# Attention values as the stationary operand in column tiles, an earlier last attention group, and a reordered output projection in a decoder-layer kernel

## The reference

```python
z = x @ w_in                       # q, k, v of 8 attention heads; q, k, v, o and gates of 4 mLSTM heads
s = q_a . k_a * HEAD_DIM_A ** -0.5 - slope[h] * dist          # only the 128 keys chosen per query
prob = softmax(s);  y_a = prob @ v_a                          # 8 heads of 64: 512 columns
y_m = sigmoid(o_m) * group_norm(mlstm(silu(conv(q_m)), silu(conv(k_m)), v_m, i, f))   # 4 heads of 128
mix = concat([y_a, y_m]) @ w_out                              # 1024 x 1024
x = layer_norm(alpha * x + mix, ln1)
ffn = hierarchical_moe(x)          # a router chooses 2 of 32 experts per token
x = layer_norm(alpha * x + ffn, ln2)
return x + sigmoid(x @ w_g) * (p @ w_p)
```

## Time and profile before

| what | value |
|---|---|
| three executions | 720.65, 721.0, 724.42 us; median 721.0 us |
| profiled execution | 722.4 us, of it 720.6 us span |
| PE busy | 648.5 us, 90% of the span |
| DVE busy | 348.8 us, 48% |
| ACT, POOL busy | 178.9 us, 168.3 us |
| mean granted TensorE clock | 0.957 of full speed |
| the chain that ended last | PE 64%, DMA 6%, SP queue 5%, DVE 5% of the span |
| DMA | 151.21 MB, mean 210 GB/s |

### The profile page before, as it was taken

How to read it: one execution, slowest core, us unless ns; L and a number is a source line. 1 busy time by engine, 2 the same in 40 slices (tenths; PEclk the granted TensorE clock), 3 DMA queues, 4 the chain that set the end, 5 groups by cost and what they waited for, 6 DMA issues and landing times.

```text
span 720.6 us, 10045 instructions
## 1 busy us (share of the span) xinstructions
PE 648.5 (90%) x3782; PEld 454.1 (63%) x3782; DVE 348.8 (48%) x803; ACT 178.9 (25%) x344; POOL 168.3 (23%) x175
## 2 busy tenths in 40 slices
PE   4999999999999999799626999999999997868997
PEld 3768887878787787688523555555555553423785
DVE  3379998657564576616762112211111111117846
ACT  5165132324323233410210111111111111024311
POOL 7206414001010000351103233333333332110100
PEclk9959999989999999999876999999999999998999
DMA  6402301203100500077296888999999999987003
GB/s 239 189 1 89 146 30 61 115 0 115 62 1 0 234 1 0 1 264 300 95 399 250 280 321 297 410 415 417 414 414 414 414 414 416 419 333 302 3 0 117
DMA packets 30438, 151.21 MB, mean 210 GB/s; under 512 B 7308, under 2 KB 7564, under 8 KB 16432
## 3 DMA queue, kind: packets, MB, share of 16 engines
q1 hardware_dynamic: 23984, 142.08, 49.9%
q0 software_dynamic: 6400, 8.42, 3.3%
HBM read 148.36 MB, written 14.68 MB: 226 GB/s over the span
## 4 chain that ended last, share of the span: by engine, by line
PE 64%; DMA 6%; SPq 5%; DVE 5%; issue 2%; ACT 1%; DVEq 0%; POOLq 0%; ACTq 0%
PE bank L1890 15%; PE bank L1599 9%; PE bank L1600 8%; PE bank L1601 8%; PE bank L1905 8%; SPq L449 5%; DMA raw<-in_w_exp_dram 4%; PE bank L1679 3%; PE bank L1954 2%; PE bank L1700 2%; PE bank L1880 2%; PE bank L1688 2%; PE bank L1729 1%; PE bank L1897 1%; PE bank L1720 1%
## 5 line engine op out<-in xcount | busy, mean ns | idle before, releaser
L1514 DVE COPY rows_x<-bank 128x128 f32<-128x128 f32 x40 | 11.6, 291 | 195.1 <-PE bank L1897 195.1
L1599 PE MATMUL bank<-w_hi,a_hi 128*128 128x384 f32 (+1 forms) x240 | 88.0, 367 | 5.9 <-POOL w_lo L578 2.9
L1601 PE MATMUL bank<-w_hi,a_lo 128*128 128x384 f32 (+1 forms) x240 | 86.5, 361 | 0.0
L1600 PE MATMUL bank<-w_lo,a_hi 128*128 128x384 f32 (+1 forms) x240 | 86.4, 360 | 0.0
L1599 PE MATMUL bank<-a_hi,w_hi 128*128 128x512 f32 (+1 forms) x176 | 71.1, 404 | 11.3 <-POOL w_lo L571 9.9
L666 POOL DMA_INDIRECT pair_dram<-rows_x,row_put x40 | 40.5, 1013 | 166.4 <-ACT rows_x L908 166.4
L1890 PE MATMUL bank<-raw,rows_x 128*64 128x256 f32 x544 | 65.6, 393 | 6.6 <-DMA raw<-in_w_exp_dram 5.0
L1600 PE MATMUL bank<-a_lo,w_hi 128*128 128x512 f32 (+1 forms) x176 | 69.5, 395 | 0.0
L1601 PE MATMUL bank<-a_hi,w_lo 128*128 128x512 f32 (+1 forms) x176 | 69.2, 393 | 0.0
L1890 PEld LDWEIGHTS bank<-raw,rows_x 128*64 128x64 f32 x544 | 40.2, 142 | 36.0 <-issue 14.7
L1890 PE MATMUL bank<-slots,rows_x 128*64 128x256 f32 x512 | 58.5, 380 | 3.2 <-DMA slots<-in_w_exp_dram 3.2
(11 more groups left out here) (250 smaller groups left out, 1032.6 us busy)
## 6 DMA issues: line engine op xcount, KB each, us to landing
raw<-in_w_exp_dram SPq DMA_DIRECT2D x42, 1024.0 KB, 13.1
slots<-in_w_exp_dram SPq DMA_DIRECT2D x36, 1024.0 KB, 12.1
rows_x<-in_w_exp_dram SPq DMA_DIRECT2D x12, 1024.0 KB, 13.9
raw<-in_w_in_dram SPq DMA_DIRECT2D x19, 512.0 KB, 4.0
raw<-in_w_wide_dram SPq DMA_DIRECT2D x4, 1536.0 KB, 6.8
y<-in_w_exp_dram SPq DMA_DIRECT2D x6, 1024.0 KB, 14.8
raw<-in_w_out_dram SPq DMA_DIRECT2D x4, 1024.0 KB, 9.2
raw<-pair_dram SPq DMA_DIRECT2D x4, 1024.0 KB, 9.1
```

The costliest lines, as they stand in the source:

```text
L1599: t_.matmul(o, lh, rh, start=first, stop=False)
L1600: t_.matmul(o, lh, rl, start=False, stop=False)
L1601: return t_.matmul(o, ll, rh, start=False, stop=last)
```

## The change

1. **pv.** The values (128 keys x 64 columns of one head) become stationary and the transposed probabilities move, 128 columns; the two heads go to the two column halves of the array and write the two halves of the partitions of `attn_bank`. The result comes out transposed, one column block of y for 512 tokens. There are 4 calls per group, in steps 4 and 5, in place of 8 in steps 2 to 5.
2. **normalise.** Row sums lie along partitions only before the transposition, so the probabilities are multiplied by the inverse sums before `turn`, in a new DVE function at the start of steps 1 to 4; `turn` waits for it. `attn_out` is a plain copy. The y of attention needs no `turn_y` any more.
3. **Table.** `ATTEND` is [12, 17, 22, 26].
4. **Output projection.** The quarters come as 2, 0, 1, 3. The four mLSTM blocks are turned one by one between the `token_major` blocks, which start as soon as attention's columns are split; tiles 0 and 1 are ended before tiles 2 and 3, and the transposition of a normalised tile (`turn_first`) stands between later blocks.
5. **DVE's normalisation** is written out by hand; centring and scaling are apart. The router's weights are rounded and split later. SP loads quarter 3 only after the last pv.

```diff
+        prob_t0 = scratch[:, 5120:6400]
...
-        row_sum = small[:, 8:16].rearrange("p (t h) -> p t h", h=2)
+        row_sums = [small[:, o:o + 8].rearrange("p (t h) -> p t h", h=2) for o in (8, 96)]
...
-        ATTEND = [12, 18, 24, 30]
+        ATTEND = [12, 17, 22, 26]
...
-        OUT_Q = [0, 2, 1, 3]
-        TURNS = [0, 4, 1, 5, 2, 6, 3, 7]
+        OUT_Q = [2, 0, 1, 3]
+        TURNS = [0, 1, 2, 3, 5, 4, 6, 7]
...
             for q in range(4):
+                if q == 3:
+                    sp.wait_ge(s_pv, NT * NG)
...
             pool.wait_ge(s_olo, 1)
+            pool.wait_ge(s_norm, 8 * NG)
             split_out(1)
...
+            for i in range(NG):
+                y_high(i)
+            work(NG, 0)
+            round_out(1)
+            for i in range(NG, 2 * NG - 1):
+                y_high(i)
+            round_out(2)
+            round_out(3)
+            y_high(2 * NG - 1)
...
+            def normalise(g, j):
+                hh, b = 2 * j // NT, 2 * j % NT
+                dve.wait_ge(s_exp, 8 * g + 2 * j + 2)
+                v.reciprocal(row_inv[:, b:b + 2, hh:hh + 1], row_sums[g % 2][:, b:b + 2, hh:hh + 1]).then_inc(s_yinv, 1)
+                dve.wait_ge(s_yinv, 4 * g + j + 1)
+                for e in range(2):
+                    part = prob[:, e, 0:(b + e + 1) * P]
+                    v.tensor_scalar(part, part, row_inv[:, b + e, hh:hh + 1], None, ALU.mult).then_inc(s_norm, 1)
...
-                v.reciprocal(row_inv, row_sum).then_inc(s_yinv, 1)
...
+                dve.wait_ge(s_pv, NT * (g + 1))
+                v.tensor_copy(y_a[:, g, :], attn_bank[:, :]).then_inc(s_ya, 1)
...
             def attention(g, j):
+                if 1 <= j <= 4:
+                    normalise(g, j - 1)
...
+            for i in range(NG):
+                y_low(i)
+            lstm_variance(HM - 1)
+            for i in range(NG, 2 * NG - 1):
+                y_low(i)
+            lstm_out(HM - 1)
+            y_low(2 * NG - 1)
...
+            mixed(2, 0)
+            mixed(2, 1)
+            norm_centre(2, s_ln)
+            mixed(3, 0)
+            norm_scale(2, s_ln, s_rs)
+            low_first(1)
+            mixed(3, 1)
+            norm_centre(3, s_ln)
+            low_first(2)
+            norm_scale(3, s_ln, s_rs)
+            low_first(3)
...
             def turn(g, u):
                 U, b = 8 * g + u, u % NT
-                pe.wait_ge(s_exp, U + 1)
+                pe.wait_ge(s_norm, U + 1)
...
+            def pv(g, b):
+
+                pe.wait_ge(s_probt, 8 * g + NT + b + 1)
+                pe.wait_ge(s_evac, step_no(g, TALL + b) + 1)
+                if b == 0 and g:
+                    pe.wait_ge(s_ya, g)
                 for s in range(b + 1):
...
+                    for hh in range(2):
+                        rows = slice(hh * DA, (hh + 1) * DA)
+                        mm = t_.matmul(attn_bank[rows, b * P:(b + 1) * P], v_a[:, g % 2, s, rows],
+                                       turned(hh * NT + b)[:, s * P:(s + 1) * P], start=s == 0, stop=s == b)
...
-                    if 2 <= j <= 5:
-                        pv(g, 2 * j - 4 + e)
+                    if 4 <= j <= 5:
+                        pv(g, 2 * j - 8 + e)
...
+            pe.wait_ge(s_evac, NSTEP - 1)
+            turn_y(4)
+            work(NG, 0)
+            pe.wait_ge(s_evac, NSTEP)
+            turn_y(5)
...
+            token_major(2, 2, 0)
+            pe.wait_ge(s_ylo, 6)
+            turn_y(6)
+            token_major(2, 3, 0)
+            token_major(2, 1, 0)
             pe.wait_ge(s_ylo, 7)
...
+            token_major(0, 0, 1)
+            token_major(0, 1, 1)
             turn_y(7)
+            token_major(0, 2, 1)
             pe.wait_ge(s_ylo, NK)
...
+            mlstm_part(0)
+            token_major(0, 3, 1).then_inc(s_wo, 1)
+            mlstm_part(1)
...
+            token_major(1, 2, 2).then_inc(s_wot, 1)
+            turn_first(0)
+            token_major(3, 2, 3).then_inc(s_wot, 1)
+            token_major(1, 3, 2).then_inc(s_wot, 1)
+            turn_first(1)
+            token_major(3, 3, 3).then_inc(s_wot, 1)
+            turn_first(2)
+            pe.wait_ge(s_wrs, 2)
+            route(0)
+            turn_first(3)
```

More of the change, by code:

```diff
@@ L357, in hybrid_layer, with turned @@
         TB_FIXED, TB_REST, TB_BLOCK = 9, 8, 9
+        def turned(u):
+            hh, b = u // NT, u % NT
+            return prob_t[:, b % 2, 0:(b + 1) * P] if hh else prob_t0[:, MO[b]:MO[b] + (b + 1) * P]
         def group(m, q):
@@ L861, in _, with y_high @@
                     work(grp, j)
[L863 to L874 removed]
+            def y_high(i):
+                k = TURNS[i]
+                if k < NG:
+                    act.wait_ge(s_proj, NSTEP)
+                    act.wait_ge(s_ya, k + 1)
+                else:
+                    act.wait_ge(s_yt, i - 3)
+                a.activation(a_hi[:, k, :], y_columns(k), ACT.Copy).then_inc(s_yhi, 1)
+            for i in range(NG):
[7 more added lines that the diff above has]
+            y_high(2 * NG - 1)
             def copy_logits(half):
@@ L885, in _ @@
                              turned_1[u][:, :].rearrange("p (k c) -> p k c", k=4), ACT.Copy).then_inc(s_x1hi, 1)
+                if u == 1:
+                    act.wait_ge(s_wr, 16)
+                    act.wait_ge(s_wo, 2)
+                    a.activation(w_hi[:, WR_AT:3 * GW], wr_raw.rearrange("p k c -> p (k c)"), ACT.Copy)\
+                        .then_inc(s_wrs, 1)
                 if u == 5:
@@ L1285, in norm_apply, with norm_scale @@
                                        op1=ALU.mult).then_inc(done, 1)
+            def norm_scale(t, done, ready):
+                m = mine[:, t, :]
                 dve.wait_ge(done, 2 * t + 1)
@@ L1297, in turned_low, with mixed, low_first @@
                     .then_inc(lo, 1)
-            def norm_tiles(prepare, ready, done, weights, banks, hi, lo):
-                for t in range(NT + 1):
-                    if t < NT:
-                        prepare(t)
-                    if t:
-                        if t == 1:
-                            dve.wait_ge(weights, 32)
-                        norm_apply(t - 1, done, ready)
-                    if t >= 2:
-                        turned_low(2 * t - 4, banks, hi, lo)
-                        turned_low(2 * t - 3, banks, hi, lo)
-                turned_low(2 * NT - 2, banks, hi, lo)
-                turned_low(2 * NT - 1, banks, hi, lo)
+            def mixed(t, half):
+                dve.wait_ge(s_xn[t], 16)
+                dve.wait_ge(s_wot, 2 * t + half + 1)
+                residual(t, half)
+                dve.wait_ge(s_r, 2 * t + half + 1)
+                norm_stats(t, half, s_bn)
+                if half:
+                    norm_variance(t, s_bn, 3 * t + 2, s_ve)
+            def low_first(t):
+                for u in (2 * t, 2 * t + 1):
+                    turned_low(u, turned_1, s_x1hi, s_x1lo)
+            mixed(0, 0)
+            mixed(0, 1)
+            dve.wait_ge(s_lnw, 32)
+            norm_centre(0, s_ln)
+            norm_scale(0, s_ln, s_rs)
+            mixed(1, 0)
+            mixed(1, 1)
+            norm_centre(1, s_ln)
+            norm_scale(1, s_ln, s_rs)
+            low_first(0)
             dve.wait_ge(s_wrs, 1)
@@ L1316, in _ @@
                             w_hi[:, WR_AT:3 * GW].bitcast(F32), ALU.subtract).then_inc(s_wrs, 1)
-            def mixed(t):
-                dve.wait_ge(s_xn[t], 16)
-                for half in range(2):
-                    dve.wait_ge(s_wot, 2 * t + half + 1)
-                    residual(t, half)
-                    dve.wait_ge(s_r, 2 * t + half + 1)
-                    norm_stats(t, half, s_bn)
-                norm_variance(t, s_bn, 3 * t + 2, s_ve)
-            norm_tiles(mixed, s_rs, s_ln, s_lnw, turned_1, s_x1hi, s_x1lo)
+            mixed(2, 0)
[9 more added lines that the diff above has]
+            low_first(3)
             n = [0]
@@ L1789, in token_major @@
                     k = 4 * (q % 2) + kk
+                    if place == 0 and t == 2:
+                        pe.wait_ge(s_ylo, k + 1)
                     mm = three(o[:, :], a_hi[:, k, t * P:(t + 1) * P], a_lo[:, k, t * P:(t + 1) * P],
@@ L1842, in turn_logits, with turn_first @@
                     mm.then_inc(s_rp, 1)
-            for t in range(NT):
+            def turn_first(t):
                 pe.wait_ge(s_ln, 2 * t + 2)
                 turn_tile(t, turned_1, s_x1t, s_x1lo)
-                if t == 2:
-                    pe.wait_ge(s_wrs, 2)
-                    route(0)
+            token_major(1, 2, 2).then_inc(s_wot, 1)
[8 more added lines that the diff above has]
+            turn_first(3)
             turn_logits(0)
```

115 lines of the change are left out of this document (37 added, 78 removed).

## The result

The change made the kernel slightly slower, by 0.4%. Over 22 executions of each, the median is 726.8 us against 723.0 us for the kernel before; the ratio is 1.0043, with a 95% interval of 1.0027 to 1.0059. In the 22 the kernel before lies 2 us above the median of the first three. 713.0 us and a gain of 8 had been forecast, with a range up to 720.5.

What follows compares the result with a forecast made beforehand. PE was taken to bound the last three projection groups, with waits on DVE behind them. The four stretches summed, +11.4 - 16.7 + 4.0 - 6.8 = -8.1 us, taking the 721.0 us median to 713.0, range 706.5 to 720.5.

Steps and rivals of the forecast that it cites:

- P: The last three projection groups, 121.98 to 278.78 us: forecast to grow by 11.4 us.
- The rival that two tiles would not overlap: In pv, column-tile records follow each other at 0.108 us, so nothing is gained: 720.6 us, no change; chance 0.08.
- A: Behind the last projection, up to w_out: 22.82 us becomes 6.1, a gain of 16.7.
- N: The first normalisation, behind w_out until turn_first of tile 3: 13.85 us becomes 7.1, a gain of 6.8.
- Waits in P: In the last three projection groups, turn waits for normalise's reciprocal and scalings: +5.5 us, bounds 2 and 12.
- Step 16: In the projection, step 15 to 16: a wait of 1.6 us appears if the low-clock stretch that hides it goes.
- The 0.5 us booked as a gain: In the last three projection groups, lstm_qk's wait on convolve_end goes, no longer colliding with attn_out: -0.5 us.
- O: The output projection w_out, to 345.73 us: 44.13 us becomes 48.1, +4.0; POOL's later power costed at nothing.
- The other term of O: In w_out, PE waits 1.6 us for the split of mLSTM block 2.
- The clock: Low-clock stretch in the last three projection groups costs 3.4 us; its going gains 3.4, another one costs 3.4.
- Waits at all 16 turning steps: Normalise finds no cover in the projection, 1.15 us a step: 18.4 in place of 5.5, 725.9 us; chance 0.07.
- Small delays eat it: Another low-clock stretch (3.4 us), DVE late in more steps (2 to 4), quarter 3 or POOL late (2): 717.5 to 724.5; chance 0.08.

Runs made afterwards that it cites:

- the power edit: Changed kernel, but POOL takes the last mLSTM head's power before splitting w_out's second quarter: 0.9978 to the kernel before, 720.9 us.
- pv first alone: Changed kernel with pv ahead of and between the two transpositions of step 4, nothing else: 0.9921 to the kernel before.
- the three edits: Changed kernel with POOL's power before the split, pv ahead of and between step 4's transpositions, convolution end behind attention in steps 9 and 16: 0.9801, 710.6 us.
- the convolution edit: Changed kernel with the power edit, plus DVE's end of a convolution behind attention in steps 9 and 16: 0.9926 to the kernel before.

## Why the prediction was wrong

**PE's work: right.** P grew by 155.3 - 149.6 = 5.7 us without waits and clock. The forecast's terms without the 0.8 of waiting were 9.7 - 0.8 - 3.3 = 5.6. pv in column tiles ran at the pace taken, 0.06 us a record: 28 records from 295.76 to the next instruction at 297.44.

```profile
295.76 1.75 PE L1748 MATMUL bank<-raw,pa 128*64 128x128 f32 x28
297.44 0.66 PE L1820 MATMUL bank<-ident,y 128*128 128x128 f32 x4
```

The rival that two tiles would not overlap is out. The Trainium skill, TensorEngine Tiling (Array Packing), Performance Considerations, has this swap with column tiles; the trace agrees as far as these records go, 40 records of 0.060 in place of 40 of 0.108 for a group (which the prediction names for the gain, have no untiled record beside them and show none). What a switch costs cannot be told apart here: the 0.4 and 0.3 us taken for it are shown by no run alone, only P's sum of 5.7 for 5.6 is.

**A and N: right**, 5.5 for 6.1 and 7.2 for 7.1.

**Waits in P: right in kind, too small, and wrong in one reason.** Normalise's waits are 7.5 us, not 5.5 (the steps that the prediction lists add up to 5.3). Steps 24, 27, 29 and 30 came as computed (0.76, 0.35, 0.82, 1.18 for 0.7, 0.4, 0.7, 1.2), steps 13 and 21 were longer (0.75 for 0.3, 1.90 for 1.4), steps 18 and 25 did not come at all. Step 16, put at nothing as long as a low-clock stretch hides it, had 1.76 in the first profile and 0.21 in the second of the same kernel, where such a stretch lies ahead. The 0.5 us booked as a gain because `lstm_qk` and `attn_out` no longer collide did not come; the wait is 0.73 in the first profile, and the second has none. And the 0.82 of the copy, which I took from the kernel before as given, was one of the cheapest things to remove.

**O: the step that failed.** The sentence was: "POOL's `power` of the last head now stands behind a `split_out` of 4.6 us; ... and POOL is through at about 16, so I cost it at nothing". I looked only at who waits for POOL's result. POOL's split starts 0.7 us before DVE's last variance instruction, and the two cannot run at once. Cost: 5.26 - 1.61 = 3.7 us of waiting, and 3.4 us of low clock behind it in the first profile, 1.7 in the second; the power edit gave 6.3 and 5.1 us back against them, of the 6.6 by which O missed. The price could have been read from the kernel before. POOL splits there, and DVE scales 128x384, then 128x512 (a third row, L966 at 8.39 with two SBUF inputs, took 2.57 us, to 1.1 us behind the end of a split, where the last of its kind took 1.21):

```profile
116.29 1.31 POOL L578 TENSOR_TENSOR w_lo<-raw,w_hi 128x512 fp32r<-128x512 f32 x1
```

```profile
116.40 1.42 DVE L1062 TENSOR_SCALAR raw<-raw 128x384 f32<-128x384 f32 x1
117.74 0.41 DVE L1062 TENSOR_SCALAR raw<-raw 128x512 f32<-128x512 f32 x1
```

The narrower operation took 1.42 us beside POOL, the wider one 0.41 behind it. The other term of O, 1.6 us for block 2, was right: 1.61 once POOL was out of the way.

**The clock: a bound that was too narrow.** I let it vary by one stretch. It cost 5.3 us more over the span: 1.7 in P and 3.4 in O, while the 3.4 that N had before moved behind it. In the changed kernel's first profile every such stretch in P and O begins inside a wait of PE or at most 1.3 us behind one. But fewer waits did not bring fewer of them by themselves: pv first alone has 5.8 us of waits in P in place of 12.1 and lost 36.2 us to the clock over its span, against 36.4 and 34.7 in the two profiles of the changed kernel. Its gain of 6.4 to 7.2 us has waits of 6.3 us beside it against the first profile and of 3.6 against the second; that it brought more than its waits is not shown.

**The rivals.** None was right. Waits at all 16 turning steps did not come. "Small delays eat it" is nearest, but it had 2 us for POOL or a late load, where POOL alone cost 3.7 us, and 5.1 to 6.3 with the clock; and its upper end of 724.5 was 2 us over what its own delays add up to (3.4 + 4 + 2). The range was also narrower than the terms allowed: the waits had 12 us as their upper bound, which with one more low-clock stretch gives 722.9, and 720.5 was stated. With the three edits the sum of the prediction would nearly hold, 708.7 us of span against 712.5, but luck is in it: 3.5 of the 3.8 us below are clock losses smaller than those of the kernel before.

What stays open: what decides where a low-clock stretch begins in P, and the worth of the convolution edit. What the table costs alone is not known either: the kernel before with [12, 17, 22, 26] and nothing else deadlocks, its engines wait for each other without end, so it has no time.

## What to carry to other kernels

When an instruction of POOL is moved, read not only who waits for its result but what DVE executes while it runs: a small DVE instruction on the critical path, of one of the two forms above, pays POOL's whole remaining length. The trace of the kernel before is the place to look for the price. When a wait on an engine's queue stays after the waiting instruction was moved, the queue is late and not the instruction; fill the wait from the waiting engine's side, with work that is ready (here pv), before trimming the queue. And compare waits only together with the clock: here their sum stayed within 2.5 us in the profiles with the old step 4, while the waits went from 8.2 to 12.1 us and the clock from 5.1 to 8.5.

## What was not expected of the hardware

- A DVE instruction of 0.17 us took 3.82 us, to the end of a POOL instruction that had begun 0.7 us before it; in two forms (scalar operation out of SBUF, and two SBUF inputs). An aggregation (0.38), a subtraction with one PSUM operand (0.69) and a scalar operation of 128x1 (0.15) were not slowed.
- Low-clock losses in P were 1.7 us in the least of these profiles and 8.5 in the worst, and one kernel had 5.1 us of them once and 6.9 us another time.
- Scalings of one column take 0.209 us on the mean, those of 512 columns 0.480: nearly half of what the widest cost is there with one column too.
